# The WKV recurrence of an RWKV layer in seven ticks a chunk, with straight and crossed 64x64 products side by side

## The reference

```python
def step(S, inp):
    r_t, w_t, k_t, v_t, a_t, b_t = inp
    sa = jnp.einsum('bhij,bhj->bhi', S, a_t)
    S = S * w_t[:, :, None, :] + sa[..., None] * b_t[:, :, None, :] + v_t[..., None] * k_t[:, :, None, :]
    return S, jnp.einsum('bhij,bhj->bhi', S, r_t)
...
y = wkv7_scan(heads(r), heads(decay), heads(k), heads(v), -kk, kk * a_h)
...
bonus = jnp.sum(heads(r).astype(jnp.float32) * heads(k).astype(jnp.float32) * r_k, axis=-1, keepdims=True)
y = y + (bonus * heads(v).astype(jnp.float32)).reshape(B, T, C)
return (y.astype(h.dtype) * g) @ w_o
```

## Time and profile before

| | us |
|---|---|
| median of 3 runs | 2232.9 |
| lowest, highest | 2229.7, 2233.21 |
| the profiled execution | 2233.94 |
| its span | 2232.2 |
| PE busy | 1951.6 (87%) |
| DVE busy | 1332.9 (60%) |
| ACT busy | 821.8 (37%) |
| POOL busy | 631.8 (28%) |

### The profile page before, as it was taken

The page is one execution under the profiler, slowest core; times in us unless marked ns, Lnnn a source line. Parts: engine busy times, 40 slices in busy tenths (PEclk is TensorE's granted clock), DMA queues, the critical chain, the costliest instruction groups (busy, mean ns, idle before and its releaser), DMA issues.

```text
span 2232.2 us, 31714 instructions
## 1 busy us (share of the span) xinstructions
PE 1951.6 (87%) x12383; PEld 1433.6 (64%) x12383; DVE 1332.9 (60%) x2201; ACT 821.8 (37%) x1267; POOL 631.8 (28%) x612
## 2 busy tenths in 40 slices
PE   6999868876766677679999999999999999989999
PEld 4997834422222222226888788988888888778887
DVE  4877685666556665545545856465546644575554
ACT  2345432211222112213444562245445444564443
POOL 1000276677777777773000000003000000001000
PEclk9999988999999999999999999999999999989999
DMA  9972499999999999996655230035555455423553
GB/s 352 348 253 94 152 354 372 387 354 358 376 364 367 359 357 362 363 387 207 208 187 182 86 103 3 4 115 180 183 187 165 153 188 188 151 76 124 196 188 113
DMA packets 255571, 510.43 MB, mean 229 GB/s; under 512 B 14810, under 2 KB 173228, under 8 KB 252380
## 3 DMA queue, kind: packets, MB, share of 16 engines
q0 software_dynamic: 74416, 270.83, 32.4%
q1 hardware_dynamic: 177898, 233.95, 31.8%
q10 hardware_dynamic: 3138, 4.00, 0.6%
HBM read 507.68 MB, written 1.05 MB: 228 GB/s over the span
## 4 chain that ended last, share of the span: by engine, by line
PE 55%; POOL 22%; issue 8%; DVE 7%; DMA 4%; ACT 3%; another core or an unknown queue 1%; SPq 0%; DVEq 0%; ACTq 0%; POOLq 0%
PE bank L639 22%; POOL big L1687 21%; PE bank L667 11%; PE bank L409 10%; PE bank L2164 5%; DMA big<-in_peer_v,aux 2%; PE bank L369 1%; DVE w_lo L319 1%; PE bank L1595 1%; DMA big<-in_w_mod 1%; PE bank L682 1%; ACT w_hi L315 1%; DMA w_raw<-in_w_in 1%; DVE big L1778 1%
## 5 line engine op out<-in xcount | busy, mean ns | idle before, releaser
L1595 PE MATMUL bank<-big 128*128 128x512 f32 x1008 | 508.7, 630 | 203.5 <-DMA big<-in_peer_v,aux 180.2
L319 DVE TENSOR_TENSOR w_lo<-w_raw,w_hi 128x2048 fp32r<-128x2048 f32 x198 | 453.6, 2293 | 274.4 <-ACT w_hi L315 274.2
L1595 PEld LDWEIGHTS bank<-big 128*128 128x128 f32 x1008 | 175.4, 193 | 515.1 <-DMA big<-in_peer_v,aux 357.0
L1778 DVE SCALAR_TENSOR_TENSOR big<-big,aux 128x1024 f32<-128x1024 f32 x256 | 313.4, 1225 | 252.6 <-DMA big<-in_peer_u,aux 231.1
L315 ACT ACTIVATE w_hi<-w_raw 128x2048 fp32r<-128x2048 f32 x198 | 378.4, 1912 | 231.3 <-PE bank L639 109.8
L1687 POOL DMA_INDIRECT big<-in_peer_v,aux x256 | 290.3, 1134 | 111.2 <-issue 75.2
L1687 POOL DMA_INDIRECT big<-in_peer_u,aux x256 | 273.2, 1067 | 103.7 <-issue 76.7
L639 PE MATMUL bank<-w_hi,hh 128*128 128x512 f32 x704 | 278.6, 396 | 2.8 <-DVE x L1466 1.7
L1672 ACT ACTIVATE big<-ident,aux 128x128 f32<-128x128 f32 x252 | 99.3, 399 | 487.5 <-PE bank L1595 247.1
L639 PE MATMUL bank<-w_lo,hh 128*128 128x512 f32 x704 | 274.2, 389 | 0.0
L639 PE MATMUL bank<-w_hi,hl 128*128 128x512 f32 x704 | 265.5, 390 | 0.0
(11 more groups left out here) (426 smaller groups left out, 2780.8 us busy)
## 6 DMA issues: line engine op xcount, KB each, us to landing
w_raw<-in_ffn_w_in SPq DMA_DIRECT2D x176, 512.0 KB
w_raw<-in_ffn_w_out SPq DMA_DIRECT2D x44, 1024.0 KB
big<-in_w_mod SPq DMA_DIRECT2D x24, 1024.0 KB, 8.1
w_raw<-in_w_in SPq DMA_DIRECT2D x22, 1024.0 KB
w_raw<-in_rwkv_w_rkv SPq DMA_DIRECT2D x12, 1024.0 KB
w_raw<-in_peer_w_query SPq DMA_DIRECT2D x8, 1024.0 KB
w_raw<-in_w_kv SPq DMA_DIRECT2D x8, 1024.0 KB
w_raw<-in_w_out SPq DMA_DIRECT2D x4, 1024.0 KB
```

What stands on the lines that cost most here:

```text
L319: dve.tensor_tensor(w_lo[i][:, :], w_raw[i][:, :], w_hi[i][:, :].bitcast(F32), ALU.subtract)\
L1595: mm = pe.matmul(bank[4 + 2 * tt + half][:, :], diag[:, turn % RROWS, :], ring_rows[turn % RROWS][:, half * 512:(half + 1) * 512], start=( ...
L1778: dve.scalar_tensor_tensor(out=row, in0=row, scalar=1.0, in1=h2tok[:, r // P, :], op0=ALU.mult, op1=ALU.mult, accum_out=dots[:, r:r + 1]). ...
```

## The change

Products are called by the name of their result. A table, `WKV_TERMS`, gives each its factors; `SWAPPED` lists the matrices that are kept with their two halves exchanged. A product whose left factor and whose bank ask for it reads one half and writes the other ("crossed", banks 2 and 3 of a group's four); the rest are "straight" (banks 0 and 1). `wkv_tick` lists seven ticks; in each, a lane of straight and a lane of crossed products run in rounds, one product (or one term of a sum) of each lane at a time, their four pairs of heads taken in turn. Each product has its own signal and its own waits (`ready`). D8 and the names of the squarings are new, the number of products is not. D2 and D4 are each copied as a pair by one ACT instruction of 128x512, N1 is copied by ACT, and E has a signal of its own. The values are turned ahead of the bonus sums, chunks 2 and 3 first; only group 1 waits for `bonus_v`; the low part of slot RKV+12 is made behind the last two inputs. The centring of y's chunks on DVE moves: chunk 0 and 1 to T1 of chunks 2 and 3, chunk 2 ahead of u1 of the last chunk. The rows of `wkv_pe` and the lists that it replaces are left out here.

```diff
+        HALF = [slice(0, DH), slice(DH, P)]
...
+        WKV_TERMS = {"D": (("be", "al"), ("al", "be")), "K": (("ka", "al"),), "RB": (("be", "rh"),), "RK": (("ka", "rh"),),
+                     "D2": (("Dt", "D"), ("D", "Dt")), "D4": (("D2t", "D2"), ("D2", "D2t")), "D8": (("D4t", "D4"),),
+                     "T1": (("D2", "T"),), "T2": (("D4", "T"),), "T3": (("D8", "T"),), "N": (("T", "E"), ("E", "T")),
+                     "N2": (("N", "N1"),), "be": (("be", "I"),), "ka": (("ka", "I"),), "x": (("K", "v"), ("al", "S")),
+                     "u": (("T", "x"),), "u1": (("N1", "u"),), "u2": (("N2", "u"),),
+                     "S": (("be_tok", "u"), ("ka_tok", "v"), ("I", "S")), "y": (("RK", "v"), ("rh", "S"), ("RB", "u"))}
+        SUMMED = ("x", "S", "y")
+
+        def wkv_terms(step):
+
+            name, c = step
+            return [t for t in range(len(WKV_TERMS[name])) if not (name in SUMMED and "S" in WKV_TERMS[name][t] and c == 0)]
+
+        def wkv_tick(c, i):
+
+            return [([("N2", c), ("be", c + 1), ("K", c + 1)], [("D", c + 1)]),
+                    ([("D2", c + 1)], [("x", c)]),
+                    ([("D4", c + 1)], [("u", c)]),
+                    ([("T1", c + 1), ("u1", c), ("D8", c + 1)], []),
+                    ([("T2", c + 1), ("u2", c), ("ka", c + 1)], []),
+                    ([("T3", c + 1), ("S", c)], [("y", c)]),
+                    ([("RB", c + 1), ("RK", c + 1)], [("N", c + 1)])][i]
+
+        def wkv_live(step):
+
+            name, c = step
+            return 0 <= c < CHUNKS - (name in ("be", "ka", "S"))
+
+        def wkv_rounds(c, i):
+
+            straight, crossed = ([(step, t) for step in lane if wkv_live(step) for t in wkv_terms(step)]
+                                 for lane in wkv_tick(c, i))
+            return [[lane[r] for lane in (straight, crossed) if r < len(lane)] for r in range(max(len(straight), len(crossed)))]
+        WKV_PE = [(step, g) for c in range(-1, CHUNKS) for i in range(7) for g in range(2)
+                  for beside in wkv_rounds(c, i) for step, t in beside if t == wkv_terms(step)[-1]]
+        ON_ACT = ("N2", "be", "ka", "D2", "D4", "D8", "x", "u", "y", "N")
...
+            def turn_values(c, ks):
+
+                for k in ks:
+                    for g in range(2):
+                        ch = slice(g * DH, (g + 1) * DH)
+                        mm = pe.matmul(bank[c][ch, k * DH:(k + 1) * DH], vT[ch, k, c * CHUNK:(c + 1) * CHUNK],
+                                       ident[ch, ch], start=True, stop=True)
+                return mm
+            third, fourth = (projection_number(RKV + 10 + j) % 2 for j in range(2))
+            pe.wait_ge(S(f"proj_free{third}"), (projection_number(RKV + 12) + 1 - third) // 2)
+            for c in (2, 3):
+                turn_values(c, range(KT - 2))
+            pe.wait_ge(S(f"proj_free{fourth}"), (projection_number(RKV + 12) + 1 - fourth) // 2)
+            for c in (2, 3):
+                turn_values(c, range(KT - 2, KT)).then_inc(S("v_turned"), 1)
+            for c in (0, 1):
+                turn_values(c, range(KT)).then_inc(S("v_turned"), 1)
...
+            def ready(step, g):
+
+                name, c = step
+
+                def act(name, c):
+                    pe.wait_ge(S("wkv_act"), wkv_count(WKV_ACT, name, c, g))
+
+                def dve(name, c):
+                    pe.wait_ge(S("wkv_dve"), wkv_count(WKV_DVE, name, c, g))
...
+                elif name == "D2":
+                    dve("D", c)
+                    act(*(("be", c) if c < CHUNKS - 1 else ("N2", c - 1)))
...
+            for c in range(-1, CHUNKS):
+                for i in range(7):
+                    for g in range(2):
+                        for beside in wkv_rounds(c, i):
+                            for step, t in beside:
+                                if t == 0:
+                                    ready(step, g)
+                            for j in range(4):
+                                for step, t in beside:
+                                    for half in range(2):
+                                        mm = wkv_product(pe, step, t, g, j, half)
+                                    if j == 3 and t == wkv_terms(step)[-1]:
+                                        mm.then_inc(S("wkv_mm"), 1)
...
+        BESIDE = {"T1": ("u1", -1), "T2": ("u2", -1), "N2": ("be", 1), "RB": ("RK", 0)}
...
+        def wkv_slot(name, g, t=0):
+
+            side = 1 if name in SECOND or (t == 1 and name not in SUMMED) else 0
+            return bank[4 * g + WKV_BANK[name]][:, side * T:(side + 1) * T]
+
+        def wkv_product(pe, step, t, g, j, half):
+
+            name, c = step
+            lhs, rhs = WKV_TERMS[name][t]
+            tok = slice(c * CHUNK, (c + 1) * CHUNK)
+            m = wkv_matrices(c, g)
+            crossing = WKV_BANK[name] >= 2
+            rows = HALF[1 - half if lhs in SWAPPED else half]
+            out_rows = HALF[half if (lhs in SWAPPED) == crossing else 1 - half]
+
+            def tile(name):
+                if name in ("al", "be", "ka", "rh"):
+                    return {"al": kkT, "be": aT, "ka": keyT, "rh": rT}[name][rows, 4 * g + j, tok]
+                if name == "v":
+                    return v_tok[rows, c, (4 * g + j) * DH:(4 * g + j + 1) * DH]
+                if name in ("be_tok", "ka_tok"):
+                    w = ("be_tok", "ka_tok").index(name)
+                    return tok_bk[rows, c % 2, w, (4 * g + j) * DH:(4 * g + j + 1) * DH]
+                if name == "I":
+                    return ident[rows, rows]
+                return m[name][rows, j * DH:(j + 1) * DH]
+            terms = wkv_terms(step) if name in SUMMED else [t]
+            return pe.matmul(wkv_slot(name, g, t)[out_rows, j * DH:(j + 1) * DH], tile(lhs), tile(rhs),
+                             start=(t == terms[0] and (len(terms) == 1 or j == 0)),
+                             stop=(t == terms[-1] and (len(terms) == 1 or j == 3)), skip_group_check=True)
...
+                elif name in ("D2", "D4"):
+                    pair = slice(2, 4) if name == "D2" else slice(0, 2)
+                    a = act.activation(spare[:, pair, g * T:(g + 1) * T], both, ACT.Copy)
+                elif name == "N":
+                    act.activation(m["N"], wkv_slot("N", g, 0), ACT.Copy)
+                    a = act.activation(m["N1"], wkv_slot("N", g, 1), ACT.Copy)
...
+            for step, g in WKV_DVE:
+                name, c = step
+                if g == 0 and step == ("T1", 2):
                     y_centre(dve, 0)
+                if g == 0 and step == ("T1", 3):
                     y_centre(dve, 1)
-                if step == ("chain", CHUNKS - 1, 3):
+                if g == 0 and step == ("u1", CHUNKS - 1):
                     y_centre(dve, 2)
-                for g in range(2):
...
+                m = wkv_matrices(c, g)
+                if name == "D":
+                    dve.wait_ge(S("wkv_mm"), wkv_count(WKV_PE, "D", c, g))
+                    dve.tensor_tensor(heads(m["Dt"]), heads(wkv_slot("D", g, 0)), each(up16), ALU.mult).then_inc(S("wkv_dt"), 1)
+                    v = dve.tensor_tensor(heads(m["D"]), heads(wkv_slot("D", g, 1)), each(low16), ALU.mult)
+                elif name == "E":
+                    if c == 0:
+                        dve.wait_ge(S("w_lo"), RKV + 14)
+                    v = dve.tensor_tensor(heads(m["E"]), heads(wkv_slot("D", g, 1)), each(low_far), ALU.mult)
...
-            act.wait_ge(S("w_lo"), RKV + 14)
-            for c in range(CHUNKS):
-                act.wait_ge(S("v_turned"), c + 1)
+            act.wait_ge(S("w_lo"), RKV + 13)
+            for i, c in enumerate((2, 3, 0, 1)):
+                act.wait_ge(S("v_turned"), i + 1)
                 act.activation(v_tok[:, c, :], bank[c][:, :], ACT.Copy).then_inc(S("v_tok"), 1)
...
             dve.tensor_tensor(aT, aT, growth, ALU.mult).then_inc(S("wkv_in"), 1)
-            lo.upto(RKV + 13)
             dve.wait_ge(S("decays"), 2)
             dve.wait_ge(S("bonus_rk"), 1)
             dve.tensor_tensor(rT, rT, hf[:, :, :], ALU.mult).then_inc(S("wkv_in"), 1)
             dve.wait_ge(S("decays"), 3)
             dve.scalar_tensor_tensor(out=kkT, in0=kkT, scalar=-1.0, in1=sig, op0=ALU.mult, op1=ALU.mult)\
                .then_inc(S("wkv_in"), 1)
+            lo.upto(RKV + 13)
             dve.wait_ge(S("v_turned"), CHUNKS)
```

More of the change, by code:

```diff
@@ L1927, in build_program @@
[L1927 to L1946, removed]
+        HALF = [slice(0, DH), slice(DH, P)]
+        SWAPPED = ("D", "Dt", "D2", "D2t", "D4", "D4t", "D8", "T", "E", "x")
+        WKV_TERMS = {"D": (("be", "al"), ("al", "be")), "K": (("ka", "al"),), "RB": (("be", "rh"),), "RK": (("ka", "rh"),),
[5 rows of a table added]
@@ L1948, in masks_pool, with wkv_count @@
+        ON_ACT = ("N2", "be", "ka", "D2", "D4", "D8", "x", "u", "y", "N")
+        WKV_ACT = [(step, g) for step, g in WKV_PE if step[0] in ON_ACT]
```

(26 more changed lines are left out.)

225 lines of the change are left out of this document (99 added, 126 removed).

## The result

The kernel after takes 2227.94 us (median of 7 runs, 2223.09 to 2231.36) where the one before takes 2233.21 in the same session; the ratio of the two is 0.9959, 95% interval 0.9944 to 0.9974. That is faster by 0.4%: some 9 us by the ratio, 5.3 by the two medians, 5.9 by the spans of the two profiled executions. It is not the 36 forecast, and lies above the upper end of the range, 2219. The profiled execution took 2228.06 us with a span of 2226.3.

The account below looks back on a forecast made before the run. TensorE was taken as the bound: a recurrence of 70.7 us of rounds plus 5.2 of waits, 33.3 less than 109.2, and 2.7 at the start made 36.0 off 2233.9; predicted 2198 us, range 2190 to 2219.

Parts of the forecast that it names:

- Four quadrants at once: Recurrence on TensorE: a straight and a crossed product share a round of 0.465 us, saving 29.8 us of 100.5.
- B: Rival on PE's pace of issue in the recurrence: 25 ns a record, about 2218 us; chance 0.10.
- the forecast's own signs: Record pace in recurrence windows: 20 to 23 ns where ticks mix if right, 29 means no sharing, over 29 slower.
- C: Rival of no sharing in the recurrence: straight and crossed products take turns, 2226 us; chance 0.08.
- Waits: PE's waits for ACT and DVE between products of the recurrence: 5.2 us, bounds 2 and 10.
- The start: Ahead of the recurrence: its first group need not wait for bonus_v and starts 2.7 us sooner, without a slow clock.
- Behind it: Work following the recurrence: nothing gets shorter, and all of the gain reaches the end.

Follow-up runs that it names:

- e1: The kernel after with the products of the second half (partitions 64 to 127) of every recurrence step left out: recurrence 77.6 us, 2207.34 us in all.
- e9: The kernel after with every product straight, the turning of y too: recurrence 106.0 us, ratio to before 0.9969.
- e8: The kernel before with the head of the change alone, products straight and in their old order: recurrence 107.1 us, ratio to before 0.9993.
- e5: The kernel after with the second half left out only for the last of the four heads of every product: recurrence 94.9 us.
- e6: The kernel after with K and RK as one product of 128 columns: recurrence 102.0 us, ratio to before 0.9965.
- e11: The kernel after with K and RK as one product and identity times S as one of 256 columns: recurrence 98.6 us, ratio to before 0.9929.
- e3: The complete kernel after with 864 more, already satisfied waits in PE's stream: recurrence 135.3 us.
- e7: The kernel after with K and RK merged, identity times S as one product per half, and first-half turnings as transposes: recurrence 105.5 us, ratio to before 1.0079.
- e4: The kernel before with the products of the second half of every recurrence step left out: recurrence 184.1 us, 2313.66 us in all.

## Why the prediction was wrong

*Four quadrants at once* was right. A shared round without a gap takes 0.476 us where the sum had 0.465. Between pauses 126 records take 2.31 us, 18 ns each, and inside shared rounds they start each 15 to 17, where the sum had 14.5. So B's 25 ns is refuted. The Trainium skill's floor of about 25 ns for short products (TensorE: Matmul & The Clock Gate, section Back-to-back issue gap) does not hold for products that share the array; the 16 ns disagree. By the forecast's own signs the result would have been C: 29 ns a record in every window, and its 2226 us lies 2 from what was measured. That is a coincidence, since the rounds refute C.

*Waits* of 5.2 us can't be read off alone: the lists have 1.8 us for ACT and DVE in after, where a pause can hide a wait, and 2.2 in e1; e9, nearly without pauses, is 5.5 longer than 216 x 0.465. They are not what the forecast lacked. Without its 22.3 us of pauses after would have taken 82.2 at most (an estimate), 6 above my 75.9.

*The start* was right: 2.8 us sooner (2.7 forecast), no slow clock. *Behind it* was right: same durations.

*The step that failed* stands under rival B, where I read the earlier trace rows: "instructions come in 27 fetches that take 1.7% of 16 engines' 110 us, 1.1 us each, while one would be needed each 2.8 us". The 1.1 us are the time of a packet on its queue, and I took it for the time that PE must wait for a block. The turn from one block to the next has two more parts, from landing to the first record (1.36 us on average) and from there to the next fetch (1.27 us), and is 3.8 us. At this turn 27 blocks are 103 us, and with that number in the sum the forecast would have been 103 + 1 or 2 for the start and end of it, 104 to 105 in place of 75.9, and 2233.9 - 2.7 - 4.5 = 2226.7. What was in sight: 27 fetches over 110 us are one per 4.1 us, no closer than the work then asked for them (one per 3.7), so nothing showed that they could come each 2.8. A queue whose share of time is small can still be the bound, if it has one thing under way at a time.

The Trainium skill says that such fetches are mostly hidden, because instructions are dispatched more slowly than they arrive (Runtime: NRT & Kernel Launch, section Instruction fetch mechanics). It has the blocks of 16 KiB and 256 instructions, and the trace agrees with these. It disagrees with "mostly hidden": 20 pauses of 0.2 to 1.8 us in this recurrence, 22.3 us together.

What the 4.5 to 4.8 us between 109.0 and after's length are made of, by the lengths of before, e8, e9 and after: 1.9 through the head and its clock (107.1), 1.1 through ticks and copies (106.0), 1.5 to 1.8 through the crossing (104.5 and 104.2). The crossing, by which 29.8 us were to be won, won under two.

What stays open: what sets the 1.36 and 1.27 us was not tried, nor whether other traffic stretches the transfer; here DMA was at 2%.

## What to carry to other kernels

Before making an engine's stream denser, divide: instructions of the stretch by 256, times 3.8 us. If that is near the stretch's length, fewer instructions help and more work side by side does not: here wider products (one for two that share a left factor, one of 256 columns for four) took 5.6 us off the recurrence, the crossing 1.5 to 1.8. Idle time put down to "issue" in pauses with 256 instructions (up to 128 records) between them is its sign. A run that drops instructions and keeps the rest tells it from a slow array, but read the length of the rounds beside it: in e1 and e5 it changed too. And 3.8 us is the turn of these runs, with little other DMA traffic; take it from the trace at hand where it shows pauses.

## What the runs showed of the hardware

- Fetches of PE's instructions, 256 of them in 16384 bytes, came each 3.80 to 3.96 us on average, and never two less than 3.2 us apart, in seven kernels on three chips (before, after, e5, e6, e8, e9, e11).
- Two straight and two crossed 64x64 products run in four quadrants at once: a round of 32 records took 0.476 us in after, the same round with straight ones alone 0.933 (e9).
- A satisfied wait that is an instruction of its own cost PE 44 ns in rounds of one product and 86 in shared rounds (e3).
- Transposes and products of the same size in turn took 143 ns a record at a granted clock of 1.00 and 213 at 0.50 (e7), against 30 at 1.00 for products alone (after).
- With one quadrant at work PE's granted clock fell to 0.50 and stayed to the end of the recurrence (e4); with two it was 1.00 (e9 throughout, before from 1360.3 on).
